# Weight streaming in a mixture-of-experts layer: the four down chunks of a pass loaded through ScalarE's DMA queue

## What is computed

```python
logits = (x @ w_router + b_router).astype(jnp.float32)
top_v, top_i = lax.top_k(logits, TOP_K)
gates = jax.nn.softmax(top_v, axis=-1)
...
for e in range(N_EXPERTS):
    hid = x @ w_up[e] + b_up[e]
    x_glu = jnp.minimum(hid[..., ::2], SWIGLU_LIMIT)
    x_lin = jnp.clip(hid[..., 1::2], -SWIGLU_LIMIT, SWIGLU_LIMIT)
    act = x_glu * jax.nn.sigmoid(SWIGLU_ALPHA * x_glu) * (x_lin + 1.0)
    out = out + gate_full[:, e:e + 1] * (act @ w_down[e] + b_down[e])
```

## Time and profile before

| what | value |
|---|---|
| median of three runs | 1157.05 us (1155.19 to 1160.03) |
| profiled execution, its own time | 1156.45 us |
| its span, from first to last instruction | 1154.7 us |
| granted TensorE clock, mean over the span | 0.984 |
| PE, DVE, ACT, POOL busy | 1055.1, 346.6, 197.7, 90.7 us |
| moved by DMA over the span | 427.40 MB, 370 GB/s in the mean |
| issues of `ring<-in_w_up_dram`, `ring<-in_w_down_dram` | 254 and 120, each of 1024 KB |
| median time from issue to landing, up and down | 25.2 and 23.2 us |

### The profile page before, as it was taken

How to read it: one execution, slowest core, us unless ns; L and a number is a source line. 1 busy time by engine, 2 the same in 40 slices (tenths; PEclk the granted TensorE clock), 3 DMA queues, 4 the chain that set the end, 5 groups by cost and what they waited for, 6 DMA issues and landing times.

```text
span 1154.7 us, 14809 instructions
## 1 busy us (share of the span) xinstructions
PE 1055.1 (91%) x5295; PEld 457.3 (40%) x5295; DVE 346.6 (30%) x784; ACT 197.7 (17%) x370; POOL 90.7 (8%) x48
## 2 busy tenths in 40 slices
PE   5998997999999999999999999999999999999996
PEld 5998955433333333333333333333233333233333
DVE  7379528422222222222222222222222211111113
ACT  4384411111111111111111111111111111111011
POOL 6563305000000000000000000000000000000000
PEclk7999998999999999999999999999999999999998
DMA  6444586799899999999999999999999999999993
GB/s 197 147 145 147 187 358 251 290 379 421 344 410 422 422 421 422 422 421 422 422 421 422 422 422 421 422 422 422 421 422 422 422 422 421 421 422 422 422 422 137
DMA packets 73399, 427.40 MB, mean 370 GB/s; under 512 B 8033, under 2 KB 21377, under 8 KB 24129
## 3 DMA queue, kind: packets, MB, share of 16 engines
q1 hardware_dynamic: 71840, 426.67, 90.3%
q10 hardware_dynamic: 1536, 0.43, 0.2%
HBM read 426.02 MB, written 1.05 MB: 370 GB/s over the span
## 4 chain that ended last, share of the span: by engine, by line
PE 53%; DMA 24%; DVE 11%; SPq 8%; issue 2%; ACT 1%; DVEq 0%; ACTq 0%
DMA ring<-in_w_up_dram 23%; PE bank L1334 22%; PE bank L1390 13%; SPq L316 8%; PE bank L1121 4%; PE bank L1299 4%; PE bank L1150 2%; DVE wbuf L1040 2%; PE bank L1375 1%; DVE wbuf L1035 1%; PE bank L1307 1%; DVE wbuf L1044 1%; PE bank L1344 1%; DVE wbuf L1034 1%; DVE ring_r L701 1%
## 5 line engine op out<-in xcount | busy, mean ns | idle before, releaser
L1334 PE MATMUL bank<-ring,wbuf 128*64 128x512 f32 x2032 | 460.4, 595 | 28.4 <-DMA ring<-in_w_up_dram 28.4
L1334 PEld LDWEIGHTS bank<-ring,wbuf 128*64 128x64 f32 x2032 | 140.2, 137 | 323.4 <-issue 226.1
L1390 PE MATMUL bank<-ring,wbuf 128*64 128x512 f32 x960 | 217.5, 595 | 0.0
L1034 DVE TENSOR_SCALAR wbuf<-bank 128x256 f32<-128x256 f32 x64 | 26.9, 420 | 360.9 <-PE bank L1334 360.9
L1390 PEld LDWEIGHTS bank<-ring,wbuf 128*64 128x64 f32 x960 | 66.7, 137 | 124.5 <-issue 124.4
L1025 DVE TENSOR_SCALAR hT<-iota_s,hT 128x64 f32<-128x64 f32 x62 | 12.9, 251 | 342.2 <-PE bank L1334 342.2
L639 ACT ACTIVATE wbuf<-wbuf 128x256 f32<-128x256 f32 x64 | 26.6, 416 | 506.2 <-DVE wbuf L1034 506.2
L1012 DVE TENSOR_TENSOR wbuf<-wbuf,bank 128x512 f32<-128x512 f32 x124 | 76.7, 680 | 0.0
L440 POOL TENSOR_TENSOR wbuf_r<-wbuf,wbuf_r 128x2048 fp32r<-128x2048 f32 x13 | 62.0, 4769 | 54.9 <-ACT wbuf_r L490 43.5
L1314 PE MATMUL bank<-wbuf,putT 64*128 64x512 f32 x264 | 65.6, 615 | 0.7 <-ACT wbuf L649 0.7
L1299 PE MATMUL bank<-X,hT 128*64 128x512 f32 x256 | 63.7, 619 | 2.5 <-DVE bsel L957 2.5
(11 more groups left out here) (249 smaller groups left out, 739.6 us busy)
## 6 DMA issues: line engine op xcount, KB each, us to landing
ring<-in_w_up_dram SPq DMA_DIRECT2D x254, 1024.0 KB, 25.2
ring<-in_w_down_dram SPq DMA_DIRECT2D x120, 1024.0 KB, 23.2
wbuf<-in_w_in_dram SPq DMA_DIRECT2D x13, 1024.0 KB, 5.2
wbuf<-in_w_out_dram SPq DMA_DIRECT2D x2, 2048.0 KB, 7.8
wbuf<-in_w_down_dram SPq DMA_DIRECT2D x4, 1024.0 KB, 6.6
mixa<-in_w_up_dram SPq DMA_DIRECT2D x2, 1024.0 KB, 14.1
mixa<-in_w_down_dram SPq DMA_DIRECT2D x2, 1024.0 KB, 8.1
cat<-in_w_down_dram SPq DMA_DIRECT2D x2, 1024.0 KB, 9.7
```

The lines of the kernel that those rows point to most:

```text
L1334: ins = mm(bank[n][c * SLOTS:(c + 1) * SLOTS, :], xT[:, k, :], wk[:, c * FF + n * 512:c * FF + (n + 1) * 512], start=(k == 0), stop=(k == ...
L1390: ins = mm(bank[2][c * SLOTS:(c + 1) * SLOTS, :], actT[:, at:at + SLOTS], wk[:, a * D + c * 512:a * D + (c + 1) * 512], start=(i == 0 and ...
```

## The change

From pass 3 on, SyncE issues only the eight up chunks. ScalarE issues the four down chunks of the next pass, all four together, when this pass has used its d3, ahead of its copy into `ysb`. The down chunks of pass 3 are issued so at the end of pass 1 (the ring slots 7 to 11 stay free in pass 2, which reads the side buffers), those of pass 4 at the end of pass 3, and so on; pass 2 issues none. In ScalarE's program passes 1 and 2 are therefore written out ahead of its loop, which reads the next expert's number from `plan` at its start.

```diff
@@ -376,9 +376,8 @@
             for c in range(SIDE):
                 replaces(1, c)
                 load_chunk(sp, 2, c)
-            for c in range(SIDE, CHUNKS):
-                replaces(1, c)
-                load_chunk(sp, 3, c)
+            replaces(1, SIDE)
+            load_chunk(sp, 3, SIDE)
             for c in range(SIDE):
                 replaces(2, c)
                 load_chunk(sp, 3, c)
@@ -386,7 +385,7 @@
             npass = sp.value_load(plan[0:1, NPASS:NPASS + 1], min_val=NE, max_val=NPASS - 1)
             with sp.Fori(4, npass) as p:
                 e = sp.value_load(plan[0:1, bass.ds(p, 1)], min_val=0, max_val=NE - 1)
-                for c in range(CHUNKS):
+                for c in range(UPC):
                     replaces(p - 1, c)
                     load_chunk(sp, e, c)
             for t in range(TT):
@@ -632,7 +631,7 @@
-            def expert_pass(p, last=False):
+            def expert_pass(p, following, last=False):
                 for n in range(2):
                     act.wait_ge(s["glu_ready"], 2 * p + n + 1)
                     w = slice(n * 256, n * 256 + 256)
@@ -646,6 +645,9 @@
                 if not last:
                     tokens_in(p + 1)
                 act.wait_ge(s["chunk_used"], (p + 1) * CHUNKS)
+                if following is not None:
+                    for c in range(UPC, CHUNKS):
+                        load_chunk(act, following, c)
                 a.copy(ysb, bank[2][:, :]).then_inc(s["y_ready"], 1)
@@ -655,10 +657,13 @@
-            expert_pass(0)
-            with act.Fori(1, last_pass) as p:
-                expert_pass(p)
-            expert_pass(last_pass, last=True)
+            expert_pass(0, None)
+            expert_pass(1, 3)
+            expert_pass(2, None)
+            with act.Fori(3, last_pass) as p:
+                e = act.value_load(plan[0:1, bass.ds(p + 1, 1)], min_val=0, max_val=NE - 1)
+                expert_pass(p, e)
+            expert_pass(last_pass, None, last=True)
```

## The result

The changed kernel takes 1166.71 us (median of five runs, 1164.08 to 1170.13) against 1157.14 us before (five runs). The ratio is 1.0081 with a 95% interval of 1.0051 to 1.0112: slower by 9.6 us, where 10.8 us were forecast. The profiled execution took 1165.72 us, its span 1163.9 us, 9.2 us more than before.

A forecast was written before the change was run, and what follows sets the result against it. TensorE was taken to set the pace first, then the DMA queue at 422 GB/s; idle time 4.8 plus order 6.0 made 10.8 us, forecasting 1167.9 us (0.93% slower), range 1160 to 1178 us.

The forecast's parts named there:

- What bounds the kernel: TensorE sets the pace first; from the first chunk wait in pass 11, the DMA queue at 422 GB/s until the last pass.
- Part 1: End of pass 3: down chunks issued later leave DMA idle from 316.0 to 321.3 us, costing 4.8 us once.
- Part 2: Down chunks in another queue take half the DMA engines, 2.4 chunks get ahead of u7, costing 6.0 us once.
- Part 3: ScalarE's four issues ahead of the copy into `ysb` end it about 1.3 us later, hidden; cost 0.
- The last pass: From u0's start at 1109.77 to the end nothing changes, as u7's data is there in time; cost 0.
- Order of issue: Rival, 10%: engines serve loads as issued whatever the queue, so only pass 3's idle time remains; 1161.9 us.
- Two queues faster or slower together: Two rivals on both queues holding work: faster, 10%, 1153 us; slower or up chunks get most, 12%, 1178.7 us if 2% slower.
- u7 about 5 us behind u6: Sign within a pass: u6 and u7 arrive about 5 us apart instead of 2.5, TensorE waiting mainly at u7.
- First wait near pass 6: Sign: TensorE's first wait for a chunk comes near pass 6 instead of pass 11.
- Landing of down loads near 15 us: Sign: median time from issue to landing of down loads falls from 23.2 us to about 15.
- A steady period of 29.8 us: Sign: the pass period in the DMA-bound regime stays 29.8 us, unchanged.

The follow-up runs named there:

- sp_late: Kernel before, all loads in SyncE's queue in the old order, but a pass's four down loads wait together for d3 of the pass before; 1161.64 us, ratio 1.0027.
- warm_u7: Changed kernel with six dummy 128x128 matmuls ahead of u7 in passes 3 to 30, to keep TensorE's clock up; 1170.69 us, ratio 1.0098.
- copy_first: Changed kernel with ScalarE's copy into `ysb` made ahead of the four down issues; 1166.39 us, ratio 1.0065.
- act_from5: Changed kernel, but SyncE still issues the down chunks of passes 3 and 4 as slots come free, ScalarE from pass 5 on; 1166.5 us, ratio 1.0079.

## Why the prediction was right, point by point

- **What bounds the kernel.** Held. DMA has work all the time from pass 4 on, at 422 GB/s, and TensorE's start of pass 31 is set by the chunks' arrival.
- **Part 1, idle time, 4.8 us.** Held: 4.3 us by the end of DMA in the changed kernel and 4.4 in sp_late, 3.8 by TensorE in sp_late. The place was right too (318 to 322.3 us). That the same delay at the end of pass 1 would be covered held: 3 us of thin traffic there went into the idle time from 291 to 295, where the changed kernel moves 391 GB/s.
- **Part 2, order, 6.0 us.** The mechanism and the half share held, the size was too large: 5.0 us in the mean of the changed kernel (3.9 at the mark of pass 31 alone) and 5.2 in warm_u7. The term that was mis-sized is the start of the down loads, "move bytes 0.85 us later, at 1.2 us". The 0.85 was read where the engines were idle; behind a busy queue it is 3.3 us or a little more, in all 27 passes. With 3.3, 13.1 - 0.34 - 3.3 = 9.5 us are shared, which gives 4.7 us. With 4.3 for part 1, the sum is 9.0 us, near the 9.4 of the mean and the 9.6 of the medians. That the late start is what makes 5 of the 6 us is worked out so; no run changes it by itself.
- **Part 3, ScalarE, 0.** Held, by copy_first, and TensorE waits for the copy no longer than before. The four issues took 1.84 us, not 1.3.
- **The last pass, 0.** Held: from the bias of pass 31 to the end of the span it is 43.2 us in both kernels.
- **The rivals.** Order of issue: excluded, since the two queues are served half and half. Two queues faster or slower together: excluded, the rate is 422 GB/s in both kernels.
- **What the trace was to show.** u7 about 5 us behind u6: 4.97. First wait near pass 6: pass 7. Landing of down loads near 15 us: 13.7. A steady period of 29.8 us: wrong, and this is the one thing that I had not seen. The mean is that (from 435.38, the bias of pass 8, to 1092.45, that of pass 30, 29.87 us), but single passes take 27.7 to 32.9 us. The down loads are issued when TensorE is done with a pass. After a long pass they are issued late, so fewer are ahead of the next u7, and that pass is short. This cause is argued from the traces, not tested alone. The swing moves the mark of any one pass by some 2 us. Read at pass 30, the loss of the changed kernel is 1092.45 - 1081.65 - 0.96 = 9.8 us instead of 8.3 (the kernel before first, then the changed one; 0.96 is what they differ by at pass 1):

```profile
1081.65 0.60 PE L1344 MATMUL bank<-wbuf,bsel 128*64 128x512 bf16 x4
1092.45 0.60 PE L1349 MATMUL bank<-wbuf,bsel 128*64 128x512 bf16 x4
```

At single marks the terms therefore don't add up to better than 2 us: sp_late and act_from5 sum to 10.4 us, of which 2.3 are idle time in act_from5 too, and the changed kernel has 8.3. In the means they do: 3.9 of sp_late and the order of 5.2 in act_from5 make 9.1 us, and the changed kernel has 9.4.

## What to carry to other kernels

- With a stream that runs at the DMA limit, don't ask how long a load takes but how many bytes are ahead of the one that is waited for. A second queue on the same engines added no rate here (422 GB/s with one and with two); it replaces an order that you chose by turns.
- If later, less urgent loads go to a second queue, they take half of the engines from the urgent ones. Here that was paid once, as lead, and not in each pass; it shows as the pass in which the waits begin.
- Look for idle DMA time at the start of such a stream, while compute still sets the pace: 5 us there were worth 5 us at the end, though no engine waited for a load within 200 us of it.

## What was unexpected of the hardware

- A load issued on ScalarE's queue while SyncE's had several chunks on their way moved its first packet 3.25 to 3.75 us after the issue, in 27 of 27 passes, against 0.6 to 1.6 us with idle engines. The Trainium skill (DMA: Bandwidth & Descriptors, "Latency and other measured facts") gives 0.6 us to the first byte of such a load; behind a busy queue the measurement differs. Where this time goes was not tried.
- TensorE's clock fell to 0.50 after some waits of 2.2 to 3.0 us at u7 and not after others (u7 at 508.80 and 1075.41, after 3.04 and 3.03 us, ran in 1.94 us). It cost nothing here, as DMA set the pace (warm_u7: the order term is 5.2 us without the slow blocks, 5.0 with them).
